# Another turn of the prompt, another order of key steps, and value steps behind weight tiles in one decoder step

## The chip, the core and the metric

The kernel runs on one core of a Trainium2 chip. The metric is the device time of one execution in microseconds (us). The engines are TensorE (PE, matrix products), VectorE (DVE), ScalarE (ACT), GpSimd (POOL) and SyncE (SP), which here only issues DMA transfers. Each engine runs its instructions in order and waits for the others on semaphores.

## What is computed

One layer of a decoder for a prompt of 512 tokens and 8 samples with one new token each, all in fp32, width 1024:

```python
mod = silu(c) @ w_ada + b_ada                      # shift, scale, gate, for each sequence
h = rms_norm(x, norm_g) * (1 + scale) + shift
aq, ak, av, az, mqk, mv, mo, mz, mif, ga, gm = split_columns(h @ w_in)
ya = attend(aq, ak, av)        # 8 heads of 64; samples: 2048 cached positions in pages of 128
ym, ... = mlstm_branch(mqk, mv, mo, mif, ...)      # 4 heads, convolution, matrix memory
ya = (ya * silu(az)) @ w_att
ym = (ym * silu(mz)) @ w_mlstm
u = sigmoid(ga) * ya + sigmoid(gm) * ym
y = x + gate * (u @ w_out)     # then a final RMSNorm
```

The attention takes, for each query, its own block of 256 keys and up to three past blocks, chosen by the query's product with the mean key of each block. For the samples the keys and values come from a paged cache (8 samples, 16 pages each).

## The kernel before, in words

**Weight tiles.** Every product with a weight matrix goes by tiles of 128 output columns. fp32 is split into a high and a low part of a shorter format. A tile's way is: SyncE issues it into one of four buffers `wraw` (L375, 512 KB); ScalarE rounds it to `wH` (`high`, L930, two halves); GpSimd takes the difference `wL` (`low`, L1362, two halves); TensorE runs 144 matmuls on it (`ztile`, L535: activation high and low by weight high, high by weight low). `wH` and `wL` have two buffers each. Tiles are numbered through: T_ATT+4t+j is tile j (q, k, v, gate) of head pair t, T_ML+8h+j is tile j of mLSTM head h.

**The prologue.** SyncE brings x, c, and seven blocks of 2 MB through two buffers: w_ada in six blocks (L405), and one block of w_in; block i waits until block i-2 has been used. Then four weight tiles with blocks between them. TensorE turns the conditioning (L556), multiplies it by block 0 (`modulation(0)`, L564), turns the biases (L579), the prompt (L586, 32 transposes, once VectorE has scaled x by its inverse norm, L1566 and L1567), the samples (L590) and the convolution state (L595), then come modulations 1, 2 and 3 and short turns of their results (L572). Scale and shift come from blocks 0 to 3; they make h, of which the first tile needs the first part (L1592, L1597).

**The attention.** Four pairs of heads, t = 0 to 3 (a loop over the last three). TensorE runs in each pair the four tiles, scores of two heads (L625), transposes of the weights (L632) and the weighted sums (L638). VectorE masks the scores and takes maxima (`causal_max`, L1656 to L1661), ScalarE exponentials and row sums (L1036), VectorE the inverse (`inverse_sums`, L1665), ScalarE the weights (L1043). Beside it the samples' keys go by in eight key steps a pair: SyncE issues the four pages of a step into one of four slots (L391, L392; a slot is free once the step before in it has been summed), a product with the query (VectorE L1675 for steps 0, 1, 2, 4, 6; GpSimd L1404 for 3, 5, 7) and a sum on VectorE (L1679).

**The mLSTM part.** Four heads of eight tiles. Beside them eight value steps a head: GpSimd multiplies a step of pages (L1435), VectorE sums over two steps (`value_pair`, L1830 and L1835). Per head VectorE also runs the convolutions (L1752, L1755), which the products of L745 read. Head 0 is written out; the others run in a loop, whose order of low parts and value steps is the same as head 0's but for the start.

All orders are written by hand, a queue for each engine; what stands behind a waiting instruction on its engine waits too. The functions that the diff touches, and the calls around them:

## Time and profile before

| | us |
|---|---|
| median of 3 runs | 772.33 |
| lowest and highest of them | 770.95, 774.32 |
| the profiled execution | 777.77 |
| its span, first to last instruction | 776.0 |
| TensorE busy | 693.6 (89%) |
| VectorE busy | 490.8 (63%) |
| GpSimd busy | 463.8 (60%) |
| ScalarE busy | 332.7 (43%) |

The mean granted TensorE clock over the span is 0.945 of full speed. HBM traffic is 186 GB/s in the mean. A chain that ended last is followed back from the last instruction; TensorE holds 55% of it, "issue" 12%, VectorE 11%, GpSimd 10%. An idle stretch of an engine is put down to what came last of all that it waited for. "x32" behind a row means that so many like instructions are merged in it.

### The profile page before, as it was taken

What the parts mean: (1) busy time and instruction counts of PE and PEld (TensorE: products, weight loads), DVE (VectorE), ACT (ScalarE), POOL (GpSimd) and SP (SyncE); (2) the same over time, 40 slices, a digit from 0 to 9 for tenths busy, and PEclk for the clock granted to TensorE, in tenths of its full rate; (3) what the DMA queues carried; (4) which work ended last, traced back from release to release, by engine and by line L of the source; (5) the groups of instructions that cost most, each with busy time, mean ns of one, the idle gap of its engine ahead of it and who ended that gap; (6) DMA issues with size and microseconds to landing.
All of it is one profiled execution on the core that took longest, in us unless ns stands there. A gap on an engine that the chain in (4) does not pass through costs nothing.

```text
span 776.0 us, 14947 instructions
## 1 busy us (share of the span) xinstructions
PE 693.6 (89%) x5066; PEld 625.8 (81%) x5066; DVE 490.8 (63%) x483; ACT 332.7 (43%) x737; POOL 463.8 (60%) x294
## 2 busy tenths in 40 slices
PE   2669999799897987958999999999889999999992
PEld 0546888578786985948999999999889998999992
DVE  0340279989899875679379488499864448533222
ACT  4253273544537153633346355453322224233554
POOL 4021148357373951868858958958395657666652
PEclk9979699789999998988999999999999999999997
DMA  8693855688888892077568658749437355733102
GB/s 314 201 356 118 256 152 163 192 258 262 263 252 276 263 268 82 8 224 211 163 204 245 208 167 248 240 149 273 109 105 202 111 151 163 242 106 88 55 0 110
DMA packets 156902, 144.69 MB, mean 186 GB/s; under 512 B 7547, under 2 KB 115152, under 8 KB 156852
## 3 DMA queue, kind: packets, MB, share of 16 engines
q1 hardware_dynamic: 142696, 136.10, 58.2%
q10 hardware_dynamic: 14164, 8.07, 3.4%
q8 instruction: 22, 0.36, 0.2%
q14 instruction: 20, 0.16, 0.1%
HBM read 135.10 MB, written 9.11 MB: 186 GB/s over the span
## 4 chain that ended last, share of the span: by engine, by line
PE 55%; issue 12%; DVE 11%; POOL 10%; DMA 4%; SPq 4%; ACT 2%; POOLq 0%; DVEq 0%; ACTq 0%
PE ps L535 42%; POOL sb_wL L1362 4%; POOL sb_arenaA L1404 4%; DVE sb_arenaA L1830 3%; DMA sb_arenaA<-in_w_ada 3%; SPq L391 2%; POOL sb_arenaA L1435 2%; SPq L392 2%; PE ps L784 2%; PE ps L564 2%; DVE sb_arenaB L1835 1%; PE ps L870 1%; PE ps L572 1%; DMA sb_wraw<-in_w_in 1%; PE ps L586 1%
## 5 line engine op out<-in xcount | busy, mean ns | idle before, releaser
L1362 POOL TENSOR_TENSOR sb_wL<-sb_wraw,sb_wH 128x512 fp32r<-128x512 f32 (+1 forms) x176 | 224.1, 1289 | 184.6 <-ACT sb_wH L930 168.6
L535 PE MATMUL ps<-sb_hH,sb_wH 128*128 128x260 f32 x1152 | 243.6, 293 | 18.4 <-POOL sb_wL L1362 14.4
L535 PE MATMUL ps<-sb_hL,sb_wH 128*128 128x260 f32 x1152 | 236.5, 288 | 0.0
L535 PE MATMUL ps<-sb_hH,sb_wL 128*128 128x260 f32 x1152 | 236.4, 287 | 0.0
L535 PEld LDWEIGHTS ps<-sb_hH,sb_wH 128*128 128x128 f32 x1152 | 183.6, 195 | 29.6 <-issue 26.0
L930 ACT ACTIVATE sb_wH<-sb_wraw 128x512 fp32r<-128x512 f32 (+1 forms) x176 | 103.5, 612 | 210.3 <-PE ps L535 132.9
L535 PEld LDWEIGHTS ps<-sb_hL,sb_wH 128*128 128x128 f32 x1152 | 183.1, 194 | 0.0
L535 PEld LDWEIGHTS ps<-sb_hH,sb_wL 128*128 128x128 f32 x1152 | 182.3, 193 | 0.0
L1435 POOL TENSOR_TENSOR sb_arenaA<-sb_arenaA 128x2048 f32<-128x2048 f32 x32 | 116.0, 3629 | 12.0 <-DMA sb_arenaA<-in_cache_v 10.0
L1404 POOL TENSOR_TENSOR sb_arenaA<-sb_arenaA 128x2048 f32<-128x2048 f32 x12 | 65.4, 5450 | 38.0 <-DMA sb_arenaA<-in_cache_k 38.0
L1679 DVE TENSOR_REDUCE sb_arenaA<-sb_arenaA 128x2048 f32 (+1 forms) x32 | 72.7, 2282 | 10.9 <-POOL sb_arenaA L1404 8.7
L1830 DVE TENSOR_REDUCE sb_arenaA<-sb_arenaA 128x512 f32<-128x4096 f32 x8 | 60.3, 7540 | 13.4 <-POOL sb_arenaA L1435 13.4
L1675 DVE TENSOR_TENSOR sb_arenaA<-sb_arenaA 128x2048 f32<-128x2048 f32 x20 | 52.3, 2613 | 1.2 <-DMA sb_arenaA<-in_cache_k 1.2
L935 ACT ACTIVATE sb_arenaB<-ps 128x520 f32<-128x520 f32 (+1 forms) x57 | 33.8, 593 | 15.8 <-PE ps L535 15.7
L1036 ACT ACTIVATE sb_arenaB<-ps,sb_nmx 128x512 f32<-128x512 f32 (+3 forms) x32 | 16.4, 527 | 44.2 <-DVE sb_nmx L1661 44.2
L1835 DVE TENSOR_REDUCE sb_arenaA<-sb_arenaA 128x512 f32<-128x4608 f32 x4 | 33.9, 8477 | 0.1
L1835 DVE TENSOR_REDUCE sb_arenaB<-sb_arenaA 128x512 f32<-128x4608 f32 x4 | 33.9, 8482 | 0.0
L564 PE MATMUL ps<-sb_arenaA,sb_gated 128*32 128x512 f32 x112 | 17.5, 724 | 11.0 <-DMA sb_arenaA<-in_w_ada 11.0
L2033 DVE TENSOR_TENSOR sb_arenaA<-sb_arenaA,ps 128x512 f32<-128x512 f32 x8 | 5.5, 687 | 34.6 <-PE ps L906 34.6
L535 PE MATMUL ps<-sb_uH,sb_wH 128*128 128x260 f32 x128 | 26.3, 286 | 0.0
L535 PE MATMUL ps<-sb_uL,sb_wH 128*128 128x260 f32 x128 | 25.8, 283 | 0.0
L535 PE MATMUL ps<-sb_uH,sb_wL 128*128 128x260 f32 x128 | 25.7, 282 | 0.0
(355 smaller groups left out, 967.5 us busy)
## 6 DMA issues: line engine op xcount, KB each, us to landing
sb_wraw<-in_w_in SPq DMA_DIRECT2D x64, 512.0 KB, 5.3
sb_arenaA<-in_cache_k SPq DMA_DIRECT2D x128, 256.0 KB, 3.1
sb_arenaA<-in_cache_v SPq DMA_DIRECT2D x128, 256.0 KB, 3.3
sb_arenaA<-in_w_ada SPq DMA_DIRECT2D x6, 2048.0 KB, 11.0
sb_arenaB<-in_state_C SPq DMA_DIRECT2D x8, 512.0 KB, 3.9
sb_wraw<-in_w_mlstm SPq DMA_DIRECT2D x8, 512.0 KB, 4.4
sb_wraw<-in_w_out SPq DMA_DIRECT2D x8, 512.0 KB, 3.8
...
```

The costliest lines, as they stand in the source:

```text
L535: last = mm(ps[:, 2 * s + a, 0:HALF], w[:, s, k, :], x[:, k, a * HALF:(a + 1) * HALF], start=(k == 0 and w is wH and x is xH), stop=(k == ...
L564: last = mm(ps[32 * g:32 * g + 32, bank, :], (hS if i == W_Q else cT)[:, k, :], ada[:, i % 2, k, :], start=(k < 4), stop=(k >= 4))
L930: f(wH[:, j % 2, part], wraw[:, j % 4, part], ACT.Copy).then_inc(hi_done, 1)
L935: ins = f(halves(dst), zps(j % 2), func)
L1036: last = f(prA[:, e, q, 0:(q + 1) * P], ps[:, b, c:c + (q + 1) * P], ACT.Exp, bias=nmx[:, e, q:q + 1], scale=SCALE, accum_out=rsum[:, e, q ...
L1362: tt(wL[:, j % 2, part], wraw[:, j % 4, part], wH[:, j % 2, part].bitcast(F32), ALU.subtract)\
L1404: tt(four, four, qbc[:, s // 4:s // 4 + 1, :].broadcast_to([P, STEP_PAGES, AW]), ALU.mult)\
L1435: tt(heads, heads, score[:, bass.ds((8 * h + s) * 32, 32)].unsqueeze(2).broadcast_to([P, 32, DH]), ALU.mult).then_inc(pool_mult, 1)
L1675: chain(tt(four, four, qbc[:, s // 4:s // 4 + 1, :].broadcast_to([P, STEP_PAGES, AW]), ALU.mult))
L1679: v.tensor_reduce(score[:, bass.ds((8 * t + s) * 32, 32)], page[:, s % 4, :].rearrange("p (g n) -> p g n", n=DH), AX, ALU.add)\
L1830: v.tensor_reduce(vhalf, vpairs[0], AX, ALU.add).then_inc(pair_free[0], 1)
L1835: v.tensor_reduce(vacc[e], vpairs[1], AX, ALU.add).then_inc(pair_free[1], 1)
```

## The change

- **Prologue.** Of the four scalings of x, VectorE does j = 0 and 2, ScalarE j = 1 and 3. The prompt's 32 transposes run in two parts of 16 with modulation 1 between them; the turns of biases, samples and state come behind. SyncE issues tiles 0 and 1 ahead of block 3, and every later block one tile later. ScalarE rounds tile 1 ahead of the leaving of modulation 3.
- **Attention.** SyncE's order of steps is 0, 3, 2, 1, 4, 7, 5, 6. VectorE's order in a pair is: first maxima, steps 7 (of the pair before), inverse sums, 6, 5 (of the pair before), 0, second maxima, 3, inverse sums, 1, 2, 4, output gate. GpSimd does product 3 of the same pair between low parts 0 and 1 of the next, product 7 between low parts 2 and 3, product 5 behind low part 3. The copies of the samples' columns and of the next selector move from VectorE to ScalarE (`samples_kept`). The maxima are kept in PSUM.
- **mLSTM head 0.** SyncE issues weight tile 7 ahead of value steps 4 and 5. GpSimd does low part 2 ahead of value step 4 and low part 3 ahead of value step 5. In the loop the sequence is the same, rotated; behind the last head value step 7 stands behind low part 3.

Core of the diff:

```diff
             ada_block(2)
-            ada_block(3)
             for j in range(4):
                 tile(j, T_ATT + j, w_in[:, :, (CQ, CK, CV, CZ)[j]:(CQ, CK, CV, CZ)[j] + P])
                 if j >= 1:
-                    ada_block(3 + j)
+                    ada_block(2 + j)
+            ada_block(6)
...
-                for s in range(8):
-                    if s in (2, 4):
-                        tile(1 + s // 2, n + 1 + s // 2, following(1 + s // 2, tt_))
+                for i, s in enumerate((0, 3, 2, 1, 4, 7, 5, 6)):
+                    if i in (2, 4):
+                        tile(1 + i // 2, n + 1 + i // 2, following(1 + i // 2, tt_))
                     key_pages(s, t)
...
-            for j in (0, 1, 2, 3, "v0", "v1", 4, "v2", 5, "v3", 6, "v4", "v5", 7, "v6", "v7"):
+            for j in (0, 1, 2, 3, "v0", "v1", 4, "v2", 5, "v3", 6, 7, "v4", "v5", "v6", "v7"):
...
+            def prompt_turn(ks):
+                for k in ks:
+                    if k >= 4:
+                        pe.wait_ge((xT_act, xT_dve)[k % 2], k // 2 - 1)
+                    for j in range(TT):
+                        last = tr(ps[:, 4 + k % 4, j * P:(j + 1) * P], xt[:, j, k * P:(k + 1) * P], ident[:, :])
+                    last.then_inc(t_x, 1)
+
             pe.wait_ge(consts, 2)
             modulation(0, 0)
+            pe.wait_ge(x_nrm, 2)
+            prompt_turn(range(4))
+            modulation(1, 1)
+            prompt_turn(range(4, KT))
             pe.wait_ge(ld_vec, 80)
...
+            mod_turn(1, 0, 2, 0)
+            mod_turn(2, 1, 2, 36)
...
-            mod_turn(1, 0, 2, 0)
-            modulation(1, 1)
-            mod_turn(2, 1, 2, 36)
             modulation(2, 0)
+            pe.wait_ge(v_col, 1)
...
             f(ss[:, :], rstd[:, :], ACT.Sqrt).then_inc(x_std, 1)
+            act.wait_ge(x_var, 2)
+            for j in (1, 3):
+                last = f(xt[:, j, :], xt[:, j, :], ACT.Copy, scale=rstd[:, j:j + 1])
+            last.then_inc(x_nrm, 1)
...
                 f(xT[:, k, :], ps[:, 4 + k % 4, :], ACT.Copy).then_inc(xT_act, 1)
+                if k == 2:
+                    ada_leave(1, 1, 0).then_inc(ada_ev, 1)
...
             high(0, 0, 0)
+            high(1, 1, 0)
             ada_leave(3, 1, 2).then_inc(ada_ev, 1)
-            high(1, 1, 0)
...
+            def samples_kept(i, n, t):
+
+                act.wait_ge(z_done, n + 3)
+                f(qkvS[:, i, bass.ds(t, 1), :].rearrange("p o n -> p (o n)"), ps[:, 2 * (i % 2) + 1, HALF - B:HALF], ACT.Copy)
...
             def attention(t, before):
                 n = T_ATT + 4 * t
-                if before:
-                    key_step(3, t - 1)
-                low(2, n + 2)
-                if before:
-                    key_step(5, t - 1)
-                else:
+                if not before:
+                    low(2, n + 2)
                     query_low()
-                low(3, n + 3)
-                if before:
-                    key_step(7, t - 1)
+                    low(3, n + 3)
                 low(0, n + 4)
+                key_step(3, t)
                 low(1, n + 5)
+                low(2, n + 6)
+                key_step(7, t)
+                low(3, n + 7)
+                key_step(5, t)
...
-            key_step(3, PAIRS - 1)
-            low(2, T_ML + 2)
-            key_step(5, PAIRS - 1)
-            low(3, T_ML + 3)
-            key_step(7, PAIRS - 1)
...
                 value_step(s, 0)
             low(1, T_ML + 9)
+            low(2, T_ML + 10)
             value_step(4, 0)
-            value_step(5, 0)
+            low(3, T_ML + 11)
+            for s in range(5, 8):
+                value_step(s, 0)
...
-                low(2, n + 2)
-                value_step(6, h - 1)
-                low(3, n + 3)
-                value_step(7, h - 1)
...
                 low(1, n + 9)
                 value_step(5, h)
-            low(2, T_GATE + 2)
-            value_step(6, MH - 1)
-            value_step(7, MH - 1)
-            for j in range(1, 4):
+                low(2, n + 10)
+                value_step(6, h)
+                low(3, n + 11)
+                value_step(7, h)
+            for j in range(2, 4):
                 low((j + 2) % 4, T_GATE + j + 2)
...
-            for j in range(TT):
+            dve.sem_inc(x_var, 1)
+            for j in (0, 2):
                 v.tensor_scalar(xt[:, j, :], xt[:, j, :], rstd[:, j:j + 1], None, ALU.mult)
...
-                if s in (3, 5, 7):
-                    dve.wait_ge(pool_mult, 3 * t + (s - 3) // 2 + 1)
+                if s in (3, 7, 5):
+                    dve.wait_ge(pool_mult, 3 * t + (3, 7, 5).index(s) + 1)
...
+            def output_gated(t):
+
...
             def attention(t, before):
-                n = T_ATT + 4 * t
-                if before:
-                    finish(t - 1)
-                else:
+                if not before:
                     gates_in()
                     gate_sums()
                     dve.wait_ge(t_mod, 6)
                     bias_added(slice(16, 24), 6).then_inc(mod_rdy, 1)
-                next_selector(0, t)
                 causal_max(0, t)
-                if not before:
+                if before:
+                    key_step(7, t - 1)
+                else:
                     gate_max()
+                inverse_sums(0, t)
                 if before:
                     key_step(6, t - 1)
-                inverse_sums(0, t)
-                if before:
                     key_step(5, t - 1)
-                    key_step(7, t - 1)
-                if not before:
+                else:
                     gate_stabilisers()
                     states_convolved()
                 key_step(0, t)
-                for i, src, at in ((0, qT, 3), (1, kT, 4), (2, vT, 5)):
-                    dve.wait_ge(z_free, n + at)
-                    v.tensor_copy(qkvS[:, i, bass.ds(t, 1), :].rearrange("p o n -> p (o n)"), src[:, T:NT])
                 causal_max(1, t)
-                next_selector(1, t)
-                key_products(1, t)
+                key_step(3, t)
+                inverse_sums(1, t)
+                for s in (1, 2, 4):
+                    key_step(s, t)
+                output_gated(t)
...
-            for s in (5, 6, 7):
+            for s in (7, 6, 5):
                 key_step(s, PAIRS - 1)
```

TensorE in the prologue, from the first modulation (L564) on, before (`sb_arenaB` holds the prompt, L572 turns a modulation's result):

```order
L564 MATMUL ps<-sb_arenaA,sb_gated 32x512 x8
L579 MATMUL ps<-sb_ident,sb_arenaB 128x80
L586 MATMUL ps<-sb_ident,sb_arenaB 128x128 x32
L590 MATMUL ps<-sb_ident,sb_arenaB 128x8 x8
L595 MATMUL ps<-sb_ident,sb_gated 128x24 x8
L572 MATMUL ps<-sb_groupsum,sb_gated 128x9 x4
L564 MATMUL ps<-sb_arenaA,sb_gated 32x512 x8
L572 MATMUL ps<-sb_groupsum,sb_gated 128x9 x4
L564 MATMUL ps<-sb_arenaA,sb_gated 32x512 x8
L572 MATMUL ps<-sb_groupsum,sb_gated 128x9 x4
L564 MATMUL ps<-sb_arenaA,sb_gated 32x512 x8
```

and after, where L581 is the prompt's turn, L591 the biases', L594 the samples', L601 the state's:

```order
L564 MATMUL ps<-sb_arenaA,sb_gated 32x512 x8
L581 MATMUL ps<-sb_ident,sb_arenaB 128x128 x16
L564 MATMUL ps<-sb_arenaA,sb_gated 32x512 x8
L581 MATMUL ps<-sb_ident,sb_arenaB 128x128 x16
L591 MATMUL ps<-sb_ident,sb_arenaB 128x80
L594 MATMUL ps<-sb_ident,sb_arenaB 128x8 x8
L572 MATMUL ps<-sb_groupsum,sb_gated 128x9 x8
L601 MATMUL ps<-sb_ident,sb_gated 128x24 x8
L564 MATMUL ps<-sb_arenaA,sb_gated 32x512 x8
L572 MATMUL ps<-sb_groupsum,sb_gated 128x9 x4
L564 MATMUL ps<-sb_arenaA,sb_gated 32x512 x8
```

The prompt's transposes stand in two parts around the second L564, and the two L572 of modulations 1 and 2 stand together.

GpSimd from the end of pair 0 into the loop over the other pairs, before (L1362 is a low part, L1404 a key product):

```order
L1362 TENSOR_TENSOR sb_wL<-sb_wraw,sb_wH 128x512 x6
L1423 UNCONDITIONAL_BRANCH
L1423 ISA
L1404 TENSOR_TENSOR sb_arenaA<-sb_arenaA 128x2048
L1361 ISA
L1362 TENSOR_TENSOR sb_wL<-sb_wraw,sb_wH 128x512
L1361 REGISTER_ALU
L1362 TENSOR_TENSOR sb_wL<-sb_wraw,sb_wH 128x512
L1401 ISA
L1404 TENSOR_TENSOR sb_arenaA<-sb_arenaA 128x2048
L1361 ISA
L1362 TENSOR_TENSOR sb_wL<-sb_wraw,sb_wH 128x512
```

and after, where L1381 is a low part and L1423 a key product:

```order
L1381 TENSOR_TENSOR sb_wL<-sb_wraw,sb_wH 128x512 x4
L1423 TENSOR_TENSOR sb_arenaA<-sb_arenaA 128x2048
L1381 TENSOR_TENSOR sb_wL<-sb_wraw,sb_wH 128x512 x4
L1423 TENSOR_TENSOR sb_arenaA<-sb_arenaA 128x2048
L1381 TENSOR_TENSOR sb_wL<-sb_wraw,sb_wH 128x512 x2
L1423 TENSOR_TENSOR sb_arenaA<-sb_arenaA 128x2048
L1441 UNCONDITIONAL_BRANCH
L1441 ISA
L1381 TENSOR_TENSOR sb_wL<-sb_wraw,sb_wH 128x512
L1380 REGISTER_ALU
L1381 TENSOR_TENSOR sb_wL<-sb_wraw,sb_wH 128x512
L1420 ISA
```

The first pair's three products now stand in the first pair, each behind two or one low parts of the next; before, they opened the loop's pass.

GpSimd in mLSTM head 0, before (L1435 is a value step, L1429 a causal mask):

```order
L1362 TENSOR_TENSOR sb_wL<-sb_wraw,sb_wH 128x512 x8
L1429 AFFINE_SELECT sb_arenaB<-sb_arenaB 128x4x128
L1362 TENSOR_TENSOR sb_wL<-sb_wraw,sb_wH 128x512 x2
L1435 TENSOR_TENSOR sb_arenaA<-sb_arenaA 128x2048 x4
L1362 TENSOR_TENSOR sb_wL<-sb_wraw,sb_wH 128x512 x2
L1435 TENSOR_TENSOR sb_arenaA<-sb_arenaA 128x2048 x2
```

and after (L1453 is a value step, L1447 the mask):

```order
L1381 TENSOR_TENSOR sb_wL<-sb_wraw,sb_wH 128x512 x8
L1447 AFFINE_SELECT sb_arenaB<-sb_arenaB 128x4x128
L1381 TENSOR_TENSOR sb_wL<-sb_wraw,sb_wH 128x512 x2
L1453 TENSOR_TENSOR sb_arenaA<-sb_arenaA 128x2048 x4
L1381 TENSOR_TENSOR sb_wL<-sb_wraw,sb_wH 128x512 x4
L1453 TENSOR_TENSOR sb_arenaA<-sb_arenaA 128x2048
L1381 TENSOR_TENSOR sb_wL<-sb_wraw,sb_wH 128x512 x2
L1453 TENSOR_TENSOR sb_arenaA<-sb_arenaA 128x2048 x3
```

Low part 2 (the second half of x4) moved ahead of value step 4, low part 3 stands between 4 and 5, and steps 6 and 7 come out of the loop behind it.

## Rows read from the trace of the kernel before

**Rows 1.** TensorE's waits, whole span: line, waited for; us, times, longest us.
```profile
PE ps L535 <- POOL sb_wL L1362: 14.4, 3, 9.1
PE ps L564 <- DMA sb_arenaA<-in_w_ada: 11.0, 2, 8.2
PE ps L632 <- ACT sb_arenaB L1043: 10.6, 5, 3.4
...
PE ps L586 <- DVE sb_arenaB L1567: 4.4, 1, 4.4
```

**Rows 2.** The chain that ended last, 0 to 60 us: start us, us, what.
```profile
20.66 2.74 DVE sb_arenaB L1566 x4
...
24.20 5.46 PE ps L586 x32
...
31.75 1.90 PE ps L564 x16
...
33.66 8.08 DMA sb_arenaA<-in_w_ada
...
41.78 3.51 PE ps L564 x16
...
51.04 7.93 PE ps L535 x48
```

**Rows 3.** DMA engines' busy tenths, 10 to 60 us in 40 slices of 1.25.
```profile
DMA  9999999998999600000269999999999999999991
```

**Rows 4.** Windows: length, then busy (x) of PE, PEld, DVE, ACT, POOL; PEclk, DMA, GB/s.
```profile
97.00:140.00 43.00, 42.34 (x300) 36.02 (x299) 37.26 (x45) 20.31 (x45) 29.15 (x11) 1.00 0.60 168
140.00:180.00 40.00, 34.98 (x185) 25.60 (x184) 36.65 (x31) 22.03 (x50) 18.73 (x9) 0.83 0.73 221
```

**Rows 5.** Timeline of TensorE: start us, us, engine, line, operation, names, shapes.
```profile
111.18 0.51 PE L535 MATMUL ps<-sb_hH,sb_wH 128*128 128x260 f32 x2
...
160.22 0.59 PE L535 MATMUL ps<-sb_hH,sb_wH 128*128 128x260 f32 x1
...
197.75 0.51 PE L535 MATMUL ps<-sb_hH,sb_wH 128*128 128x260 f32 x2
...
240.13 0.51 PE L535 MATMUL ps<-sb_hH,sb_wH 128*128 128x260 f32 x2
```

**Rows 6.** Waits of all engines, 100 to 290 us.
```profile
ACT sb_arenaB L1036 <- DVE sb_nmx L1661: 39.7, 7, 12.8
...
DVE sb_arenaA L1679 <- POOL sb_arenaA L1404: 8.7, 4, 2.2
```

**Rows 7.** Groups by line and shape, 100 to 280 us: busy us, mean ns | idle before.
```profile
L1404 POOL TENSOR_TENSOR sb_arenaA<-sb_arenaA 128x2048 f32<-128x2048 f32 x12 | 65.4, 5450 | 38.0 <-DMA sb_arenaA<-in_cache_k 38.0
...
L1679 DVE TENSOR_REDUCE sb_arenaA<-sb_arenaA 128x2048 f32 x24 | 54.4, 2281 | 6.4 <-POOL sb_arenaA L1404 4.4 <-DVE sb_arenaA L1675 2.0
L1675 DVE TENSOR_TENSOR sb_arenaA<-sb_arenaA 128x2048 f32<-128x2048 f32 x20 | 52.3, 2613 | 1.2 <-DMA sb_arenaA<-in_cache_k 1.2
...
L930 ACT ACTIVATE sb_wH<-sb_wraw 128x512 fp32r<-128x512 f32 x36 | 20.7, 620 | 19.6 <-DMA sb_wraw<-in_w_in 13.0 <-PE ps L535 5.8 <-ACT sb_kqN L1121 0.8
```

**Rows 8.** Timeline of VectorE, one product of the first pair.
```profile
126.35 6.19 DVE L1675 TENSOR_TENSOR sb_arenaA<-sb_arenaA 128x2048 f32<-128x2048 f32 x1
```

**Rows 9.** Timeline of SyncE's queue, two tile issues with eight pages between.
```profile
153.33 0.38 SPq L375 DMA_DIRECT2D sb_wraw<-in_w_in  x1
...
163.36 0.38 SPq L375 DMA_DIRECT2D sb_wraw<-in_w_in  x1
```

**Rows 10.** Timeline of GpSimd, VectorE and TensorE in head 0, 342 to 362 us.
```profile
342.46 3.62 POOL L1435 TENSOR_TENSOR sb_arenaA<-sb_arenaA 128x2048 f32<-128x2048 f32 x1 [1.00 <-DMA sb_arenaA<-in_cache_v]
346.04 2.50 POOL L1362 TENSOR_TENSOR sb_wL<-sb_wraw,sb_wH 128x512 fp32r<-128x512 f32 x2
...
346.12 7.45 DVE L1830 TENSOR_REDUCE sb_arenaA<-sb_arenaA 128x512 f32<-128x4096 f32 x1 [4.30 <-POOL sb_arenaA L1435]
...
361.14 2.32 PE L745 MATMUL ps<-sb_arenaB 128*128 128x512 f32 x8
```

More of the change, by code:

```diff
@@ L268, in decoder_step @@
         aw = sb("aw", [B, 2, MH])
-        mx = sb("mx", [P, 2, TT])
+        mx = ps[:, 6, T - TT:T]
         nmx = sb("nmx", [P, 2, TT])
@@ L574, in mod_turn @@
                 last.then_inc(t_mod, 1)
+            def prompt_turn(ks):
[5 more added lines that the diff above has]
+                    last.then_inc(t_x, 1)
             pe.wait_ge(consts, 2)
             modulation(0, 0)
+            pe.wait_ge(x_nrm, 2)
+            prompt_turn(range(4))
+            modulation(1, 1)
+            prompt_turn(range(4, KT))
             pe.wait_ge(ld_vec, 80)
-            tr(ps[:, 5, 0:V_ROWS], vrow, ident[0:V_ROWS, 0:V_ROWS]).then_inc(t_x, 1)
-            pe.wait_ge(v_col, 1)
-            pe.wait_ge(x_nrm, 1)
-            for k in range(KT):
-                if k >= 4:
-                    pe.wait_ge((xT_act, xT_dve)[k % 2], k // 2 - 1)
-                for j in range(TT):
-                    last = tr(ps[:, 4 + k % 4, j * P:(j + 1) * P], xt[:, j, k * P:(k + 1) * P], ident[:, :])
-                last.then_inc(t_x, 1)
+            tr(ps[:, 3, P:P + V_ROWS], vrow, ident[0:V_ROWS, 0:V_ROWS]).then_inc(t_x, 1)
             pe.wait_ge(xT_act, 3)
@@ L1061, in copy_out @@
                 f(qbc[:, e, :], ps[:, 4 + 3 * e, :], ACT.Copy).then_inc(qbc_rdy, 1)
+                f(selc[:, e, :], rowsel[:, bass.ds(2 * t + e + 2, 1), :].rearrange("p o n -> p (o n)"), ACT.Copy)\
+                    .then_inc(selc_rdy, 1)
+            def samples_kept(i, n, t):
+                act.wait_ge(z_done, n + 3)
+                f(qkvS[:, i, bass.ds(t, 1), :].rearrange("p o n -> p (o n)"), ps[:, 2 * (i % 2) + 1, HALF - B:HALF], ACT.Copy)
             def attention(t, before):
@@ L1067, in attention @@
                 high(2, n + 2, quad)
+                samples_kept(0, n, t)
                 leave(0, n, qT, ACT.Copy)
@@ L1077, in attention @@
                     ada_leave(6, 4, 4).then_inc(ada_ev, 1)
+                samples_kept(1, n + 1, t)
                 leave(1, n + 1, kT, ACT.Copy)
@@ L1081, in attention @@
                 weights(0, t)
+                samples_kept(2, n + 2, t)
                 leave(0, n + 2, vT, ACT.Copy)
@@ L1564, in _ @@
             chain(v.reciprocal(rstd[:, :], ss[:, :]))
-            for j in range(TT):
+            dve.sem_inc(x_var, 1)
+            for j in (0, 2):
                 v.tensor_scalar(xt[:, j, :], xt[:, j, :], rstd[:, j:j + 1], None, ALU.mult)
@@ L1568, in _ @@
             for k in range(1, KT, 2):
-                dve.wait_ge(t_x, k + 3)
+                dve.wait_ge(t_x, k + 2)
                 v.tensor_copy(xT[:, k, :], ps[:, 4 + k % 4, :]).then_inc(xT_dve, 1)
+            dve.wait_ge(t_x, KT + 2)
+            v.tensor_copy(vcol[:, :], ps[:, 3, P:P + V_ROWS]).then_inc(v_col, 1)
             dve.wait_ge(t_x, KT + 3)
@@ L1576, in bias_added @@
                           over(vcol[:, V_BA + part.start:V_BA + part.stop], 9), ALU.add)
+            dve.wait_ge(v_col, 1)
             dve.wait_ge(t_mod, 2)
@@ L1685, in key_step @@
                 key_sums(s, t)
-            def next_selector(e, t):
-                dve.wait_ge(qbc_mm, 2 * t + e + 1)
-                v.tensor_copy(selc[:, e, :], rowsel[:, bass.ds(2 * t + e + 2, 1), :].rearrange("p o n -> p (o n)"))\
-                    .then_inc(selc_rdy, 1)
-            def finish(t):
-                inverse_sums(1, t)
-                key_sums(1, t)
-                for s in (2, 3, 4):
-                    key_step(s, t)
+            def output_gated(t):
                 dve.wait_ge(z_free, T_ATT + 4 * t + 6)
```

11 lines of the change are left out of this document (4 added, 7 removed).

## The prediction

> **What bounds the kernel now.** I read TensorE's waits over the whole span first, since it is the busiest engine by far and only its idle stretches and its slow clock can be won: 14.4 us for low parts (three waits, the longest 9.1), 11.0 for blocks of w_ada, 10.6 for the normalised weights of the attention, 4.4 for the scaled prompt [rows 1]. The reader should see few, large waits at known places.
>
> Then the chain of the first 60 us [rows 2]: four scalings on VectorE, 32 transposes, one modulation, and 8.08 us in which a block of w_ada is under way. It is asked for only after the modulation before it, at 33.66, and the DMA engines stand nearly still from 27.5 to 35 [rows 3]. The first weight tile starts on TensorE at 51.04.
>
> Then the attention by stretches [rows 4]: from 97 to 140 TensorE is busy 42.34 of 43 us at full clock, from 140 to 180 34.98 of 40 at a mean granted clock of 0.83, a mix of 2.4 and 1.2 GHz. The first tile of pairs 1, 2 and 3 starts at 111.18, 160.22 and 197.75, that of the mLSTM part at 240.13 [rows 5]: periods of 49.0, 37.5 and 42.4 us. The waits of this stretch show who is late: ScalarE waits 39.7 us for VectorE's negated maxima, VectorE 8.7 for GpSimd's products [rows 6].
>
> Why VectorE is late is read from durations. A product of a key step takes 2.61 us in the mean of 20 while a sum of the same size takes 2.28 [rows 7]; one product, beside one of GpSimd's, took 6.19 [rows 8]. GpSimd's own take 5.45 in the mean of 12 [rows 7]. The two stop each other. The Trainium skill ("SBUF — State Buffer", Who interferes with whom) says why: a VectorE instruction with two SBUF inputs contends with a GpSimd one that reads SBUF, whoever issues first holds the shared ports for the whole instruction, and a reduce is never held up. The rows agree, 2.28 for all 24 sums. By that rule a change that only reorders the same products may keep every stop; what it would give is rival 2.
>
> **The prologue.** Two of the four scalings go to ScalarE. VectorE's four took 2.74 us [rows 2]; its two take 1.37, and ScalarE's two run beside them; ScalarE's passes of 512 columns take about 0.6 [rows 7], so two of 1024 make 2.4 at most. The scaled prompt is there up to 1.2 us sooner, 23.0 instead of 24.2. Then 16 transposes, half of 5.46 us, stand ahead of modulation(1), not 32 and three turns. It ran from 31.75 to 33.65; it now starts near 26.6 and ends near 28.6, so block 3 is asked for at 28.65 instead of 33.66. It no longer travels alone: tiles 0 and 1 (0.5 MB each) are issued ahead of it. Block 2 is in when the transfers stop, about 28 [rows 3]; the tiles need 3 us behind it, block 3 its 6 (2 MB at the 350 to 390 GB/s of the full slices): in at 37.5 against 41.74. Modulation(3) took 3.51 us after its wait and modulation(1) 1.90 [rows 2]; with more work ahead of it I allow 1.5 of that. The 5.8 us behind it up to the first tile stay. So 51.04 becomes 45 to 45.5: **−6**, bounds −7 and −4 (block 3 slowed by the tiles beside it).
>
> **The attention.** Moved to ScalarE: three copies of sample columns and two selectors a pair. ScalarE was busy 22.03 of 40 us [rows 4]; 1.1 us more lies beside TensorE's tiles: nothing, or 0.3 a pair where one delays a result's leaving. VectorE loses what they cost it, 2 us or so a pair, hidden or not by what it waits for.
>
> What counts is what stands in front of the maxima. Before, the first maxima of a pair stood behind the sum of step 1 and the whole of steps 2, 3 and 4 of the pair before, and the inverse sums behind step 6; now the maxima open the pair, and only the sum of step 7 stands between them and the inverse sums. The 10.6 us [rows 1] and the slow clock behind them should mostly go. The shortest pair took 37.5 us; 49.0 and 42.4 are 11.5 and 4.9 above it, and behind 240.13 TensorE still waits up to 6 us for weights and a low part. On the one hand, then, some 20 us.
>
> Against the whole of it stands SyncE. From one tile's issue to the next, with eight pages between, 10.03 us go by [rows 9]: 40.1 a pair. Three pairs then take 120.3, if SyncE isn't ahead, against 128.9: 8.6. And the products still meet: GpSimd's step 3 beside VectorE's step 0, 7 beside 1 or 2, 5 beside the next pair's 6, and who issues first decides on up to 4.5 us (the 6.19 less the 2.28, and GpSimd's share); the trace of before can't tell. I take 9 for the three pairs and 3 behind them: **−12**, bounds −16 and −3 (a stop in each pair).
>
> A wait is added on GpSimd: low part 3 of the next pair stands behind product 7, which waits for its pages; TensorE's fourth tile waits for that low part, and behind it in the queue stands product 5. By my times it is done 2 to 4 us before TensorE comes. Nothing, then; beyond that it is rival 3.
>
> **Head 0 of the mLSTM part.** Low part 2 stood behind value steps 4 and 5 and ended at 348.5; TensorE had waited 9.1 us [rows 1, 10]. It now comes well ahead, and the wait goes. What is late next: VectorE's sum over value steps 4 and 5 started at 346.12, when step 5 had ended, and took 7.45; behind it come the convolutions, and TensorE's products of L745, which read them, started at 361.14 with no wait shown [rows 10], 7.6 us after the sum's end. So the 9.1 us aren't won but move to L745. Worse, step 5 now stands behind low part 3, 2.5 us, of which the 1.00 that it waited for pages comes back: it runs 343.96 to 347.58 instead of 342.46 to 346.08. The sum ends at 355.0, L745 starts at 362.6: **+1.5**, bounds 0 (step 5 not moved) and +3 (TensorE slow after 12 us of idling: modulation(3) lost 1.6 so [rows 2]). The loop over the heads issues the same sequence, rotated: nothing. At its end value step 7 of head 3 stands behind one low part more, of 2.5 us, which it had waited for in part: **+0.7**, bounds 0 and +2.5.
>
> **Sum.** −6 −12 +1.5 +0.7 = −15.8. The profiled execution took 777.8 us (span 776.0), so 762.0; on the median of the runs, 772.33, it is 756.5.
>
> **Rivals.**
> 1. Head 0 gains too: value steps 4 and 5 come early with their pages, which no longer stand behind anything, and L745 starts with them. 7 of the 9.1 us and the 1.5 are won: −15.8 −8.5 = −24.3, 748. For it: VectorE idled 4.30 us there [rows 10]. Against it: it idled for step 5, which GpSimd's order moves back. Chance 0.12.
> 2. The products stop each other as before, or SyncE sets the pace: the attention gives 4. −6 −4 +2.2 = −7.8, 764.5. For it: the product of 6.19 us and the 40.1 a pair. Against it: the maxima stand ahead of the products in any case. Chance 0.23.
> 3. Slower. Product 7 waits for pages that SyncE can fetch only once the sum of step 3 has freed the slot; low part 3 waits behind it, and TensorE at the fourth tile of each pair. It decides from 4 us of lateness on. At 4 us beyond that, and 3 lost to the slow clock (half of the 6.8 that a clock of 0.83 costs in 40 us [rows 4]), four pairs cost 28: −6 −12 +28 +2.2 = +12.2, 784.5. For it: VectorE waited 8.7 us for GpSimd before [rows 6]. Against it: three steps of VectorE stand between that release and the need. Chance 0.06.
> 4. The tiles delay block 3 so far that the prologue gives nothing: 762.5. Chance 0.07; with rival 2 as well, 770.5, chance 0.04.
> The forecast itself has 0.48.
>
> **Numbers.** A measurement tells 0.5%, 3.9 us, from no change; 768.5 to 776.2 is the same. The forecast, rivals 1 and 2 and rival 4 alone are faster, less their small ends: 0.87. The same: 0.07. Slower: 0.06. Range 746 to 769: rivals 1, 2 and 4 in, rival 3 and the case of both out. The forecast's own would be 751 to 762.
>
> **What would show it.** Block 3 in by 38, the first tile at 45 to 46. First tiles of the pairs near 105, 146 and 186, the mLSTM part's at 226; no wait for the normalised weights over 3 us, a granted clock of 1.00 through the second and third pair. No low part waited for in head 0, and in its place one wait of 9 to 12 us at the products of L745. Heads 1 to 3 unchanged. Wrong if TensorE waits at a pair's fourth tile, if VectorE's product 0 takes over 4 us in each pair, or if the first tile stays beyond 49.

## The result

| | before | changed |
|---|---|---|
| first comparison, median | 772.61 us (4 runs) | 764.57 us (4 runs: 762.44 to 767.14) |
| ratio | | 0.9897, 95% interval 0.9857 to 0.9937 |
| second comparison, median | 775.14 us (21 runs) | 763.3 us (6 runs) |
| ratio | | 0.9845, interval 0.9803 to 0.9888 |
| profiled executions | 777.8 (span 776.0), and one of span 771.6 | 763.5 (span 761.8), and one of span 758.7 |

The change makes the kernel 8 us faster by the medians of the first comparison and 12 by those of the second; 15.8 (a ratio of 0.9795) were forecast. The spans of the profiles differ by 13 to 14 us, but executions of one kernel differ by 3 to 8 us among themselves, so that one pair of profiles can't tell 8 from 14.

TensorE's waits in the changed kernel, to be read against [rows 1] (line, what it waited for: us in total, times, longest us):

```profile
PE ps L564 <- DMA sb_arenaA<-in_w_ada: 12.3, 2, 8.3
PE ps L749 <- ACT sb_arenaB L1198: 11.7, 1, 11.7
PE ps L820 <- DVE sb_tS L1764: 7.4, 1, 7.4
...
PE ps L636 <- ACT sb_arenaB L1052: 4.0, 4, 1.6
...
PE ps L535 <- POOL sb_wL L1381: 1.1, 1, 1.1
```

The 14.4 us for low parts are 1.1, and that holds in the second profile of each kernel too (14.9 and 1.1). The 10.6 for the weights of the attention are 4.0 here, but 5.7 and 6.4 in the second profiles (e1, e2), so this drop isn't shown to be the change's. Two other waits have come: 11.7 us at the products behind the convolutions (L749, L745 before) and 7.4 us at the samples' selector products (L820).

The prologue, TensorE's timeline (start us, us, [idle before]), against [rows 2], and the DMA engines' busy tenths from 10 to 60 us against [rows 3]:

```profile
38.06 3.64 PE L564 MATMUL ps<-sb_arenaA,sb_gated 128*32 128x512 f32 x16 [4.00 <-DMA sb_arenaA<-in_w_ada]
...
46.89 0.56 PE L535 MATMUL ps<-sb_hH,sb_wH 128*128 128x260 f32 x1 [2.59 <-DVE sb_hL L1612]
```

```profile
DMA  9999999999999999999999999999999930000000
```

Block 3 comes when forecast (38.0), the gap in the transfers is gone, but modulation 3 runs slow (3.64 us at a granted clock of 0.50) behind an idle 4.0 us. The first tile starts at 46.9, not at 45 to 45.5; over the ten profiles with this order of the prologue it starts between 45.8 and 46.9.

First tiles of pairs 1, 2, 3 and of the mLSTM part, against [rows 5]:

```profile
105.38 0.51 PE L535 MATMUL ps<-sb_hH,sb_wH 128*128 128x260 f32 x2
...
142.53 0.51 PE L535 MATMUL ps<-sb_hH,sb_wH 128*128 128x260 f32 x2
...
183.18 0.39 PE L535 MATMUL ps<-sb_hH,sb_wH 128*128 128x260 f32 x1
...
228.00 0.50 PE L535 MATMUL ps<-sb_hH,sb_wH 128*128 128x260 f32 x2
```

Forecast were 105, 146, 186 and 226. The periods are 37.2, 40.7 and 44.8 us (49.0, 37.5, 42.4 before): the first is what TensorE's own work takes (37.2 in every pair of e16 below, where it waits for nothing), the others grow. What stands behind 228, VectorE's timeline and the TensorE row that waits:

```profile
243.57 6.70 DVE L1690 TENSOR_TENSOR sb_arenaA<-sb_arenaA 128x2048 f32<-128x2048 f32 x1
...
252.64 0.68 DVE L1707 TENSOR_TENSOR sb_gated<-sb_gated,ps 128x512 f32 x1
253.35 3.78 DVE L1764 TENSOR_TENSOR sb_tS<-sb_qkvS 128x32 f32<-128x32 f32 x1
```

```profile
257.18 1.06 PE L820 MATMUL ps<-sb_tS,sb_headsel 128*128 128x32 f32 x4 [7.43 <-DVE sb_tS L1764]
```

A product of 6.70 us instead of 2.28 and a product over 32 columns of 3.78 us (0.19 in e11, where GpSimd's products are short), both beside GpSimd's operations: TensorE stands behind VectorE's tail. Head 0, against [rows 10], is as forecast in kind: VectorE's sum starts when value step 5 has ended, and TensorE waits at L749:

```profile
335.25 7.32 DVE L1832 TENSOR_REDUCE sb_arenaA<-sb_arenaA 128x512 f32<-128x4096 f32 x1 [5.69 <-POOL sb_arenaA L1453]
```

```profile
349.45 4.40 PE L749 MATMUL ps<-sb_arenaB 128*128 128x512 f32 x8 [11.68 <-ACT sb_arenaB L1198]
```

### The profile page after: what moved, and what is told of

Its sections match the earlier page's. It is cut to its first block, busy times and chain, and to the rows that moved or that the text cites. A ratio compares the mean times of both kernels' runs of the same rounds, so it can differ in the third digit from the quotient of the medians.

```text
span 761.8 us, 14935 instructions
## 1 busy us (share of the span) xinstructions
PE 685.2 (90%) x5066; PEld 614.8 (81%) x5066; DVE 485.7 (64%) x461; ACT 337.7 (44%) x759; POOL 465.5 (61%) x294
## 4 chain that ended last, share of the span: by engine, by line
PE 52%; issue 12%; POOL 12%; DVE 11%; DMA 6%; SPq 3%; ACT 3%; POOLq 0%; DVEq 0%; ACTq 0%
PE ps L535 41%; POOL sb_wL L1381 5%; DMA sb_arenaA<-in_w_ada 4%; POOL sb_arenaA L1423 3%; POOL sb_arenaA L1453 3%; DVE sb_arenaA L1832 3%; SPq L391 2%; DVE sb_arenaA L1690 1%; PE ps L564 1%; PE ps L788 1%; SPq L392 1%; DVE sb_arenaB L1837 1%; PE ps L629 1%; PE ps L874 1%; DMA sb_arenaA<-in_cache_k 1%
## 5 line engine op out<-in xcount | busy, mean ns | idle before, releaser
L1381 POOL TENSOR_TENSOR sb_wL<-sb_wraw,sb_wH 128x512 fp32r<-128x512 f32 (+1 forms) x176 | 233.1, 1340 | 190.9 <-ACT sb_wH L934 176.5
L535 PE MATMUL ps<-sb_hH,sb_wH 128*128 128x260 f32 x1152 | 240.4, 290 | 4.0 <-DVE sb_hL L1612 2.8
L535 PE MATMUL ps<-sb_hL,sb_wH 128*128 128x260 f32 x1152 | 234.0, 285 | 0.0
L535 PEld LDWEIGHTS ps<-sb_hH,sb_wH 128*128 128x128 f32 x1152 | 180.7, 192 | 14.8 <-issue 13.8
L535 PEld LDWEIGHTS ps<-sb_hH,sb_wL 128*128 128x128 f32 x1152 | 180.1, 191 | 0.0
L535 PEld LDWEIGHTS ps<-sb_hL,sb_wH 128*128 128x128 f32 x1152 | 180.1, 191 | 0.0
L1453 POOL TENSOR_TENSOR sb_arenaA<-sb_arenaA 128x2048 f32<-128x2048 f32 x32 | 115.9, 3627 | 7.8 <-DMA sb_arenaA<-in_cache_v 5.8
L1423 POOL TENSOR_TENSOR sb_arenaA<-sb_arenaA 128x2048 f32<-128x2048 f32 x12 | 58.0, 4836 | 24.9 <-DMA sb_arenaA<-in_cache_k 24.9
L1690 DVE TENSOR_TENSOR sb_arenaA<-sb_arenaA 128x2048 f32<-128x2048 f32 x20 | 61.0, 3050 | 5.8 <-DMA sb_arenaA<-in_cache_k 5.7
L564 PE MATMUL ps<-sb_arenaA,sb_gated 128*32 128x512 f32 x112 | 19.1, 783 | 12.3 <-DMA sb_arenaA<-in_w_ada 12.3
```

The source lines that it names most:

```text
L535: last = mm(ps[:, 2 * s + a, 0:HALF], w[:, s, k, :], x[:, k, a * HALF:(a + 1) * HALF], start=(k == 0 and w is wH and x is xH), stop=(k == ...
L564: last = mm(ps[32 * g:32 * g + 32, bank, :], (hS if i == W_Q else cT)[:, k, :], ada[:, i % 2, k, :], start=(k < 4), stop=(k >= 4))
L1381: tt(wL[:, j % 2, part], wraw[:, j % 4, part], wH[:, j % 2, part].bitcast(F32), ALU.subtract)\
L1423: tt(four, four, qbc[:, s // 4:s // 4 + 1, :].broadcast_to([P, STEP_PAGES, AW]), ALU.mult)\
L1453: tt(heads, heads, score[:, bass.ds((8 * h + s) * 32, 32)].unsqueeze(2).broadcast_to([P, 32, DH]), ALU.mult).then_inc(pool_mult, 1)
L1690: chain(tt(four, four, qbc[:, s // 4:s // 4 + 1, :].broadcast_to([P, STEP_PAGES, AW]), ALU.mult))
```

## The experiments

All with 5 rounds; the ratio is to the kernel before, run beside it, with its 95% interval. Two ratios are "not told apart" where the interval of their quotient holds 1. Starts of tiles are read from the timeline of the profile of each; differences to "the changed kernel" go by its ratio in e2, 0.9845.

**Both kernels again.** No edit.

> The kernel before, unchanged, once more. Theory P (the forecast was made against a profiled execution 5.2 us above the median, and took away waits that a usual execution of before has only in part): its median is 771 to 773, its profiled span below 773, the stretch at a granted clock of 0.83 (140 to 180 us) is better than 0.90 here, and pair 1 to pair 2 takes under 46 us instead of 49.0. Theory Q (the profile is typical, the parts of the change give less than I worked out): the profile looks as before, 49.0 us and 0.83 again.

Measured: 775.41 us, ratio 0.9995 (0.9966 to 1.0024), span 771.6. The outcome lies between P and Q: the span fits P, the stretch from 140 to 180 us at a clock of 0.83 fits Q. The starts are 111.33, 159.10, 199.32 and 243.20: the long pair is there again (47.8 us), so it is no accident, but this execution was 4.4 us shorter in the end.

> The changed kernel, unchanged, once more. Both theories: 763 to 767, ratio 0.988 to 0.992. In the profile the pair starts stay within 2 us of 105.4, 142.5, 183.2 and 228.0, if nothing in them is left to chance; under theory P the collisions of VectorE's and GpSimd's products differ from execution to execution, and a start or two moves by 3 to 5 us.

Measured: 763.3 us, ratio 0.9845 (0.9803 to 0.9888), span 758.7, starts 105.4, 142.6, 181.5, 224.9. Two starts moved by 1.7 and 3.1 us, and the wait at L820 was 4.1 instead of 7.4. Two executions of one program part ways in the third pair. The ratio lies below the 0.988 to 0.992 that both theories gave.

**The parts.** e3 is before with the prologue's hunks alone, e4 the changed kernel with the orders of head 0 and of the heads' loop (the diff's lines with tile 7, and GpSimd's lines with value steps) as before.

> Before with the prologue's part alone. Theory Q says the prologue gives what its first tile shows, -4.2 us (51.04 to 46.89), in the end too: 768.2. Theory P says the same of the first tile; but VectorE's key steps and SyncE's pages bound the attention of before, so -4 to -6 only as far as the first page comes earlier (78.89 before). A rival to both: pages and collisions shift and give back all of it, 771 to 773.

Measured: 770.09 us, ratio 0.9935 (0.9904 to 0.9965), so −5.0; first tile at 46.9.

> Prologue and attention as changed, the weight tiles and value steps of the mLSTM heads as before. The forecast's step (+1.5 in head 0, +0.7 at the end for the part left out here) says this is 2.2 us faster than the full change: 762.4. The profiles say that the full change gained 2.1 us in head 0 and 1.1 after it: then this is 3 us slower, 767.6. In the profile the wait of 9.1 us for low part 2 stands again and the one of 11.7 us at the products behind the convolutions is gone.

Measured: 764.16 us, ratio 0.9864 (0.9828 to 0.9901). From e3 to e4 the attention's part brings 0.9864/0.9935, −5.5 us, between −1.8 and −9.2 by the two intervals. From e4 to the full change head 0's part brings 0.9845/0.9864, −1.5 us, between −5.8 and +2.8. The wait for low part 2 (9.3 us) stands again in e4, and from tile 0 of head 1 to tile 0 of head 2, the stretch beside head 0's last value steps, it takes 74.5 us, in the changed kernel 75.3 and 75.0: no gain from the wait that went. Over all profiles with before's order of the heads this stretch takes 76.1, 76.1, 72.5, 74.5, 72.2 and 72.4 us (before, e1, e3, e4, e12, e15), each with a wait of 7.0 to 9.6 for the low part.

The stretches of all profiles size the attention's part a second time. Each cell has the range and the mean in us; tile 0 of the mLSTM part is the one that follows the four pairs.

| | first tile to tile 0 of the mLSTM part | on to tile 0 of head 1 | both |
|---|---|---|---|
| before's attention (before, e1, e3) | 189.1 to 192.1, 190.2 | 79.2 to 87.5, 84.0 | 271.2 to 277.1, 274.2 |
| changed (changed, e2, e4 to e10, e13) | 177.3 to 186.3, 181.4 | 79.8 to 88.8, 83.9 | 261.9 to 268.9, 265.3 |

So some 9 us are gained in the four pairs and nothing in the stretch behind them.

**What TensorE waits for behind the change.** e5 moves TensorE's selector products behind a tile:

```diff
-            pe.wait_ge(sel_dve, 1)
-            ...  # L820, L825: headsel, turns of qkvS
             ztile(3, T_ML + 3, hH, hL)
+            pe.wait_ge(sel_dve, 1)
+            ...  # the same
```

> The changed kernel, with TensorE's selector products (L820, L825) behind weight tile 3 of the mLSTM part instead of ahead of it. Theory S (what the attention gained is partly lost because TensorE waits 4 to 7 us at L820 for the samples' products tS, which stand on VectorE behind key step 4 and the output gate): the wait shrinks to under 1 us, tile 3 starts when its low part is there, about 3 us behind tile 2, and the whole gets 3 to 5 us faster than the changed kernel, ratio to before 0.978 to 0.982. Rival (low part 3 and the tiles behind it are late anyway, SyncE issues them only after the last key page, and VectorE's last key steps set the end of this stretch): 0 to 1 us faster, the wait reappears at L833 or at the next tile's low part.

Measured: 760.89 us, ratio 0.9825 (0.9789 to 0.9861), not told apart from 0.9845. The wait at L820 is gone, and one of 5.4 us at L838, for VectorE, has come. That is what the rival said: VectorE's tail bounds this stretch, and it doesn't matter where TensorE meets it.

e6 takes the convolutions ahead of the sum in head 0:

```diff
-                if h < MH - 1:
+                if 0 < h < MH - 1:
                     value_pair(4, h, first)
...
                     convolve(1, h)
+                if h == 1:
+                    value_pair(4, 0, True)
```

> The changed kernel, with VectorE's sum over value steps 4 and 5 of head 0 moved behind the convolutions of head 1. Theory H (the 9.1 us wait of head 0 did not go but moved to the products behind the convolutions, 11.7 us, because these stand behind that sum): the wait at L749 goes almost wholly, TensorE's next tile starts when GpSimd has made its low part, 8 to 10 us sooner, and the whole gets 6 to 10 us faster than the changed kernel: 753 to 757 or a ratio of 0.972 to 0.978 to before. Rival (value steps and pages of head 1 are held up by the later release of the slots): TensorE waits in head 1 instead, gain 0 to 3 us.

Measured: 766.88 us, ratio 0.9897 (0.9865 to 0.9929). The wait at L749 is gone, and TensorE waits at the next row for a tile; SyncE's queue shows why:

```profile
349.73 1.12 PE L767 MATMUL ps<-sb_ident,sb_arenaB 128*128 128x128 f32 x4 [13.63 <-ACT sb_vS L941]
```

```profile
338.87 3.83 SPq L392 DMA_DIRECT2D sb_arenaA<-in_cache_v  x4
342.97 0.38 SPq L375 DMA_DIRECT2D sb_wraw<-in_w_in  x1
```

The tile of 342.97 stands behind four pages, and these wait for the slots that VectorE's moved sum (it ends at 338.0) frees. Theory H fell in this form; e10 adds SyncE's part:

```diff
-                for j in range(8):
-                    tile(j, n + j, ml_tile(j + 4, h) if j < 4 else following(j - 4, hh))
-                    value_pages(j, h, False)
+                def at(j):
+                    tile(j, n + j, ml_tile(j + 4, h) if j < 4 else following(j - 4, hh))
+                at(0)
+                for j in range(8):
+                    if j < 7:
+                        at(j + 1)
+                    value_pages(j, h, False)
```

> e6 (convolutions ahead of VectorE's sum over steps 4 and 5) and with it SyncE's weight tiles of heads 1 to 3 one value step earlier. In e6 the wait of head 0 had moved once more, to L767 (13.6 us), for a tile whose issue at 343.0 stood behind pages that wait for that same sum. Theory H, mended: three things stood in a row there (low part, convolutions, the issue of tile 5 of head 1), and with the third gone the wait at L767 falls from 13.6 to under 3 us; head 0's tile 0 to head 1's tile 0 takes 66 to 70 us instead of 75 to 77; 5 to 9 us faster than the changed kernel. Rival: a fourth one follows (GpSimd's low part behind a value step whose pages are late, 10 us).

Measured: 758.28 us, ratio 0.9783 (0.975 to 0.9816); the wait at that row is 4.3 us, and from tile 0 of head 1 to tile 0 of head 2 it takes 71.8 us. Three waits stood in a row in the changed kernel, and with all three gone 5 us are won against it (0.7 to 9 by the intervals). SyncE's part alone was not run, so that it needs e6 beside it is argued and not shown; and e3, e12 and e15, with none of the three edits, cross the same stretch in 72.2 to 72.5 us.

**The prologue's transfers.** e7:

```diff
             ada_block(2)
+            ada_block(3)
             for j in range(4):
                 ...
-                    ada_block(2 + j)
-            ada_block(6)
+                    ada_block(3 + j)
```

> The changed kernel, with SyncE's order of the prologue as before (block 3 ahead of tiles 0 and 1, and so on). Theory D (with the transposes in two parts the DMA engines are busy without a gap in the prologue, so the order of transfers decides; tiles 0 and 1 ahead of block 3 cost 3 to 4 us): block 3 is in at 33.5 to 34.5 instead of 38.0, the first tile starts at 43 to 44 instead of 46.9, and the whole is 2 to 4 us faster than the changed kernel. Rival (the tiles are needed just as early, and ScalarE rounds them before modulation 3 leaves): the first tile starts at 46 or later.

Measured: 759.73 us, ratio 0.9805 (0.9776 to 0.9834), 3 us better than the changed kernel, though not told apart from its 0.9845; first tile at 44.4:

```profile
34.68 1.92 PE L564 MATMUL ps<-sb_arenaA,sb_gated 128*32 128x512 f32 x16
39.89 1.87 PE L572 MATMUL ps<-sb_groupsum,sb_gated 128*128 128x9 f32 x8 [3.29 <-ACT sb_gated L975]
44.36 0.77 PE L535 MATMUL ps<-sb_hH,sb_wH 128*128 128x260 f32 x2 [2.59 <-DVE sb_hL L1612]
```

Modulation 3 now runs fast, 1.92 us at a clock of 1.00, with no idle time before it. Theory D holds for the first tile, a little short: 44.4, 44.9 and 44.0 with this order (e7, e8, e13). e9 also lets modulation 3 leave ahead of the rounding of tiles 0 and 1 (`ada_leave(3, 1, 2)` two lines up):

> e7 (block 3 ahead of the tiles) and with it ScalarE's order of before: modulation 3 leaves ahead of the rounding of tiles 0 and 1. In e7 TensorE waited 3.3 us at L572 for that leaving, which stood behind the rounding of tile 1, landed at 38.2. Theory D says now that block 3 and the tiles are both in time: first tile at 41.5 (44.4 in e7, 46.9 as changed), 2 to 3 us faster than e7. Rival: the tiles' rounding and low parts are the last thing then (tile 0 in at 36.4, rounded and its low part taken by 40), first tile at 43 or later.

Measured: 761.38 us, ratio 0.9812 (0.9765 to 0.9859): nothing more. The rival's number holds (first tile at 43 or later), its reason only in part: the result leaves earlier, and the low parts of the two tiles, which come later for it, then run on GpSimd beside VectorE's making of h. One operation of that takes 1.50 us; in e7, where the low parts end at 42.1, it takes 0.54.

```profile
39.02 1.88 PE L572 MATMUL ps<-sb_groupsum,sb_gated 128*128 128x9 f32 x8 [0.72 <-ACT sb_gated L975]
45.97 0.56 PE L535 MATMUL ps<-sb_hH,sb_wH 128*128 128x260 f32 x1 [5.07 <-DVE sb_hL L1612]
...
39.57 5.12 POOL L1381 TENSOR_TENSOR sb_wL<-sb_wraw,sb_wH 128x512 fp32r<-128x512 f32 x4 [9.99 <-ACT sb_wH L934]
...
42.07 1.50 DVE L1607 TENSOR_SCALAR sb_arenaB<-sb_arenaB,sb_hscale,sb_modT 128x512 f32<-128x512 f32 x1
```

e8 is e5, e6 and e7 in one.

> All three of these edits in one. If they are independent, the gains add up: by theories S, H and D 12 to 18 us faster than the changed kernel, 745 to 752. If they all wait for the same thing (GpSimd's order or SyncE's issues), no more than the largest of them, 755.

Measured: 762.52 us, ratio 0.984 (0.9802 to 0.9878), no faster than the changed kernel. By the medians e6 takes back what e7 gives; the wait at the row of L767 is 14.7 us there.

**The two floors.** e11 and e12 cut GpSimd's key products to 8 of 512 columns of each page (`four[:, :, 0:8]`), so the other 504 are left out. e14 and e15 leave out SyncE's read of the page number and take the pages in plain order (`bass.ds(first + i, 1)`), so the table's choice is left out, for the value pages of the mLSTM part as well as for the keys. e16 does both.

> The changed kernel, with GpSimd's products of key steps 3, 5 and 7 cut to 8 of 512 columns of each page (the rest is left out). Theory L (VectorE's and GpSimd's products stop each other, and this is what holds the attention at 41.5 us a pair): VectorE's products fall from 3.05 us to under 2.4 in the mean, the mLSTM part starts at 216 to 220 instead of 225 to 228, the whole is 6 to 9 us faster than the changed kernel. Theory F (SyncE's issues set the pace, 40.1 us a pair): under 3 us faster, VectorE waits for pages instead.

> The kernel before with the same cut (the same part left out). Theory L: 5 to 12 us faster than before, and the difference to e11 is what the order alone brings, without collisions: by my forecast's terms 12 in the attention, then, which would show that the collisions and not the order are where the gain was lost. Theory F: both gain little, and the difference between them stays at the 5 to 7 us that the attention and head 0 gave.

Measured: e11 755.1 us, ratio 0.9752 (0.9718 to 0.9787), 7 us better than the changed kernel; e12 763.49 us, ratio 0.9861 (0.9828 to 0.9893), 11 us better than before. In e12 all of VectorE's products take what a sum takes, and the long pair of before is gone (39.9 us instead of 49.0):

```profile
L1675 DVE TENSOR_TENSOR sb_arenaA<-sb_arenaA 128x2048 f32<-128x2048 f32 x20 | 45.7, 2284 | 8.2 <-DMA sb_arenaA<-in_cache_k 8.2
```

So the stops, together with the time that GpSimd spends on these products, cost 7 to 11 us in either order; the cut takes both away at once, and no run parts them. The change brings 0.9752/0.9861, 8.5 us, without them too: alone they aren't where the difference to the forecast went. The last part of theory L falls, and the mLSTM part starts at 223.2 in e11, not at 216 to 220.

> The changed kernel with the pages fetched in plain order, without reading each page's number from the page table (the pages' choice is left out; as many transfers of the same size). Theory F (SyncE's 40.1 us a pair is the floor that the new order runs into): an issue takes well under 1.17 us, the mLSTM part starts at 218 to 222 instead of 225 to 228, VectorE no longer waits for pages, 4 to 7 us faster than the changed kernel. Rival (the slots' release and the 3 us of a transfer are what GpSimd waits for): under 2 us.

> The kernel before with the same edit. Theory F: there SyncE stood idle 24 us of the attention (10 to 12 as changed), so it wasn't the floor: 0 to 2 us faster than before. Then what the change would have brought without this floor is e14 against e15: 14 to 18 us, the forecast's size. Rival: it gains as much as e14.

> The changed kernel with plain pages and with GpSimd's key products cut to 8 of 512 columns (both left out as in e14 and e11). If the two floors stand one behind the other: the pairs follow each other at 37 to 38.5 us, TensorE's own time, the mLSTM part starts at 216 to 218, 10 to 14 us faster than the changed kernel. If one hides the other, it stays at e11's 0.975.

Measured: e14 760.52 us, ratio 0.9803 (0.9783 to 0.9823), 3 us better than the changed kernel and not told apart from it, its mLSTM part at 225.7 and not at 218 to 222; e15 781.15 us, 1.0071 (1.0052 to 1.0091), 5.5 us worse than before; e16 743.64 us, 0.9586 (0.9563 to 0.9609), 20 us better than the changed kernel. Groups of 100 to 280 us, changed kernel, then e14, e15 and e16 (busy us, mean ns | idle before):

```profile
L1690 DVE TENSOR_TENSOR sb_arenaA<-sb_arenaA 128x2048 f32<-128x2048 f32 x19 | 58.7, 3090 | 5.7 <-DMA sb_arenaA<-in_cache_k 5.7
...
L1423 POOL TENSOR_TENSOR sb_arenaA<-sb_arenaA 128x2048 f32<-128x2048 f32 x12 | 58.0, 4836 | 24.9 <-DMA sb_arenaA<-in_cache_k 24.9
```

```profile
L1422 POOL TENSOR_TENSOR sb_arenaA<-sb_arenaA 128x2048 f32<-128x2048 f32 x12 | 64.3, 5361 | 0.6 <-DMA sb_arenaA<-in_cache_k 0.5
L1689 DVE TENSOR_TENSOR sb_arenaA<-sb_arenaA 128x2048 f32<-128x2048 f32 x19 | 61.8, 3252 | 0.0
```

```profile
L1674 DVE TENSOR_TENSOR sb_arenaA<-sb_arenaA 128x2048 f32<-128x2048 f32 x19 | 61.0, 3210 | 0.0
```

```profile
L1689 DVE TENSOR_TENSOR sb_arenaA<-sb_arenaA 128x2048 f32<-128x2048 f32 x19 | 46.4, 2444 | 0.0
```

With pages in time nobody waits for them (24.9 and 5.7 us become 0.6 and 0), but GpSimd and VectorE meet more often: 3.25 us a product instead of 3.09. Part of what one floor gives goes to the other. Alone they give 3 and 7 us, together 20. Half of the 20 falls behind the attention: from the first tile to the mLSTM part e16 takes 170.0 us (181.1 and 178.1 in the changed kernel), from there to tile 0 of head 1 75.1 (85.1 and 85.3), and the wait at L820 is gone. In e16 TensorE sets the pace of every pair:

```profile
142.43 0.51 PE L534 MATMUL ps<-sb_hH,sb_wH 128*128 128x260 f32 x2
...
179.59 0.51 PE L534 MATMUL ps<-sb_hH,sb_wH 128*128 128x260 f32 x2
...
216.75 0.51 PE L534 MATMUL ps<-sb_hH,sb_wH 128*128 128x260 f32 x2
```

In e15, before's order with pages in time, each period is like the long one of before (starts 111.29, 159.08, 206.58, 253.81): VectorE's products took 3.21 us instead of 2.61 [rows 7]. That long pair was the order's own rhythm, and the late pages of the later pairs had spared them the stops. e14 against e15 is 0.9803/1.0071, −21 us: that is what the whole change, its prologue included, is worth without SyncE's floor. The waits of SyncE for a slot from 80 to 260 us, before (second profile) and changed, are its slack, and show how near the floor came:

```profile
SPq L391 <- DVE sb_arenaA L1679: 24.0, 6, 8.4
```

```profile
SPq L391 <- DVE sb_arenaA L1694: 12.0, 6, 4.6
```

**The best of them.** e13 is e7 and e10 in one.

> e7 and e10 together: block 3 ahead of the tiles in the prologue, the convolutions of head 1 ahead of VectorE's sum in head 0, SyncE's tiles of heads 1 to 3 one value step earlier. If the two are independent, their ratios multiply: against the changed kernel 0.9805/0.9845 and 0.9783/0.9845, so 0.974 to before, 755. If the prologue's gain is taken back by SyncE's pages in the attention, 0.978.

Measured: 755.37 us, ratio 0.975 (0.9713 to 0.9786), as the product of the two said. It beats both kernels, the changed one by 7 us.

## Why the prediction was wrong

The time (756.5) was 7 to 8 us too low. Of 15.8 us that were forecast, 8 or 12 came, by comparison; the parts below are measured beside the second. The sign held, and so did most of the mechanism named for the prologue and that for head 0; the sum for the attention did not. By its own steps:

- **Prologue, −6, bounds −7 and −4.** −5.0 by e3, with its first tile at −4.2. Block 3 was forecast at 37.5 and came at 38.0. Mis-sized was the 1.5 us for a faster modulation 3: it stood behind an idle 4.0 us and ran slow. The forecast had the tiles' transfers ahead of block 3 as its bound; in e7, e8 and e13 they cost 1 to 3 us at the first tile, and in the whole 3 us that are not told from 0.
- **Attention, −12, bounds −16 and −3.** This is the step that failed: −5.5 by e3 and e4 (−1.8 to −9.2). The first half of it, "9 for the three pairs", is near what the profiles have: from the first tile to the mLSTM part 190.2 us in the mean became 181.4. The second half, "3 behind them", was not there: 84.0 us became 83.9. I had read TensorE's waits behind 240.13 as removable. The one for a low part (2.5 us) went, the one for weights (3.3 us) is 0.4 in the changed kernel and 2.8 in e2, and 7.4 or 4.1 us at L820 came to them; e5 shows that VectorE's tail stands behind those. I had not asked what VectorE does there: output gate and samples' products stand behind key step 4, and steps 7, 6 and 5 of the last pair still come behind them. I had also left open who would be stopped ("the trace of before can't tell"). By the means from 100 to 280 us VectorE's products lose 15.4 us to stops in the changed kernel and 14.1 in e2, against 6.6 and 6.7 in the two profiles of before; GpSimd's lose 4.0 and 7.5 against 11.4 and 9.2 (each against the shortest product, 2.28 and 4.50). The new order laid the stops on the engine that TensorE waits for. By e14 to e16 both floors hold at once, which I had priced one at a time and as alternatives: with both gone the attention and the stretch behind it give 20 us.
- **Head 0, +1.5.** The kind was right in each point: the 9.1 us moved to L745 (11.7 there), value step 5 was later. In size the ratios say −1.5, not told from 0; the stretches from tile 0 of head 1 to tile 0 of head 2 say 74.0 in the mean of six profiles with before's order of heads and 75.1 in eight with the new one (changed, e2, e5, e7, e9, e11, e14, e16), and their ranges overlap. What the slow clock costs moved along with the wait: the tile behind the old wait, at 347.44, took 8.1 us at a granted clock of 0.71, the same tile takes 6.0 at 1.00 now, and L749's products take 4.40 us at 0.55 instead of 2.32. (A tile is 48 matmuls, the x48 of [rows 2], not 144.) The stretches before, then in the changed kernel: us from and to, length, TensorE busy, granted clock, DMA share, GB/s:

```profile
347.44:355.50 8.06, 8.06 (x50) 0.71 0.57 167
```

```profile
325.90:331.80 5.90, 5.90 (x49) 1.00 0.76 246
349.40:353.90 4.50, 4.40 (x8) 0.55 0.93 279
```

- **End of the heads, +0.7.** Not seen apart by e4. From the first tile behind the heads to the end it takes 251.3 us in the mean of the six profiles with before's order of heads and 252.4 in that of the twelve others, with ranges that overlap.
- **Rivals.** Rival 1 was not it. Rival 2 (−7.8, the attention gives 4) is nearest to what was measured, with its two reasons joined. Rivals 3 and 4 were not seen: no fourth tile waited for a low part (1.1 us in all).

The rule of the Trainium skill ("SBUF — State Buffer", Who interferes with whom) that the prediction used held in every run: sums stay at 2.28 us and two-input products stretch up to 6.70. What it costs at most was measured too: 11 us before, 7 us after (e12, e11), GpSimd's own time on the products included.

Left open: why executions part from pair 3 on was not tried. The slow clock has a part in it: the last of the three periods took 49.6 us at a granted clock of 0.86 in e4 and 49.7 at 0.86 in e5, but 44.8 and 43.5 at 0.96 in the changed kernel and e2. Nor was it tried whether a larger share of the key steps on one engine would end the stops.
